# A state-space scan issued in rounds, with one bank pair for its decays and its gate units behind it

## The reference, cut to what matters

```python
def ssd_chunked(xs, dt, a, bm, cm):
    ...
    a_cs = jnp.cumsum(adt, axis=-1)
    seg = a_cs[..., :, None] - a_cs[..., None, :]
    decay_in = jnp.exp(jnp.where(tri, seg, -jnp.inf))
    cb = jnp.einsum("bclgn,bcsgn->bcgls", cc, bc)
    y_diag = jnp.einsum("bcgls,bcgrls,bcsgrp->bclgrp", cb, decay_in, xd)
    states = jnp.einsum("bclgn,bcgrl,bclgrp->bcgrpn", bc, decay_states, xd)
    def step(h, inp):
        st, dec = inp
        return h * dec[..., None, None] + st, h
    _, prev = lax.scan(step, h0, ...)
    y_off = jnp.einsum("bclgn,bcgrpn,bcgrl->bclgrp", cc, prev, jnp.exp(a_cs))
    return (y_diag + y_off).reshape(b, l, g, r, p)
...
y = y_fwd + y_bwd + d_skip * xs
return rms_norm(y * jax.nn.silu(z), ssd_norm)
```

## Time and profile before

| | us |
|---|---|
| median of 3 runs (lowest, highest) | 2350.87 (2345.1, 2355.63) |
| the profiled execution's own time | 2345.79 |
| its span, first to last instruction | 2344.0 |
| TensorE busy in the span | 2198.4 (94%) |
| ScalarE, VectorE, GpSimd busy | 1004.5, 1142.7, 962.0 |
| mean granted clock of TensorE, as a share of full speed | 0.961 |

### The profile page before, as it was taken

The page is one execution under the profiler, slowest core; times in us unless marked ns, Lnnn a source line. Parts: engine busy times, 40 slices in busy tenths (PEclk is TensorE's granted clock), DMA queues, the critical chain, the costliest instruction groups (busy, mean ns, idle before and its releaser), DMA issues.

```text
span 2344.0 us, 28202 instructions
## 1 busy us (share of the span) xinstructions
PE 2198.4 (94%) x10837; PEld 1826.0 (78%) x10848; DVE 1142.7 (49%) x1836; ACT 1004.5 (43%) x2027; POOL 962.0 (41%) x730
## 2 busy tenths in 40 slices
PE   7999899999988997899999998998899999999997
PEld 5788778888877776778888877785697887888886
DVE  3445565554344666465554363664445335544322
ACT  5666444443235555244443254655243234323222
POOL 3655553433457652444333442224323334322232
PEclk9999999999999999799999997998899999999998
DMA  4111122232213221122222221110012232222221
GB/s 157 55 55 60 49 99 99 90 108 99 94 60 102 82 68 39 62 82 90 98 100 97 88 88 36 37 36 19 19 46 101 88 108 72 92 106 90 101 99 52
DMA packets 29846, 183.08 MB, mean 78 GB/s; under 512 B 3984, under 2 KB 4112, under 8 KB 11920
## 3 DMA queue, kind: packets, MB, share of 16 engines
q1 hardware_dynamic: 29712, 181.27, 22.4%
HBM read 174.97 MB, written 2.10 MB: 76 GB/s over the span
## 4 chain that ended last, share of the span: by engine, by line
PE 82%; DVE 6%; ACT 5%; issue 3%; POOL 2%; DMA 1%; SPq 0%; POOLq 0%; ACTq 0%; DVEq 0%
PE PS L1452 81%; PE PS L1577 1%; POOL LO L2735 1%; DVE bQS L2191 1%; PE PS L1690 0%; ACT HI L1779 0%; DMA RAW<-wall 0%; DVE aQS L2191 0%; DVE T_f L2263 0%; DVE XL L2268 0%; DVE YH L2293 0%; PE PS L1625 0%; POOL cQ L2818 0%; ACT bP L1995 0%; POOL cROT L2810 0%
## 5 line engine op out<-in xcount | busy, mean ns | idle before, releaser
L2735 POOL TENSOR_TENSOR LO<-RAW,HI 128x512 fp32r<-128x512 f32 (+2 forms) x382 | 540.9, 1432 | 601.6 <-ACT HI L1779 601.3
L1452 PE MATMUL PS<-XH,HI 128*128 128x512 f32 (+1 forms) x1584 | 637.6, 403 | 24.5 <-DVE XL L2191 6.7
L1452 PE MATMUL PS<-XH,LO 128*128 128x512 f32 (+1 forms) x1584 | 624.4, 394 | 0.0
L1452 PE MATMUL PS<-XL,HI 128*128 128x512 f32 (+1 forms) x1584 | 618.1, 395 | 1.0 <-DVE XL L2268 1.0
L1779 ACT ACTIVATE HI<-RAW 128x512 fp32r<-128x512 f32 (+3 forms) x668 | 365.4, 608 | 171.3 <-PE PS L1452 168.0
L2191 DVE TENSOR_TENSOR LO<-RAW,HI 128x512 fp32r<-128x512 f32 (+2 forms) x286 | 305.0, 1071 | 246.2 <-ACT HI L1779 245.8
L1452 PEld LDWEIGHTS PS<-XH,HI 128*128 128x128 f32 (+1 forms) x1584 | 302.2, 191 | 87.7 <-issue 20.4
L1452 PEld LDWEIGHTS PS<-XH,LO 128*128 128x128 f32 (+1 forms) x1584 | 301.4, 190 | 65.7 <-issue 0.8
L1452 PEld LDWEIGHTS PS<-XL,HI 128*128 128x128 f32 (+1 forms) x1584 | 300.8, 190 | 62.7 <-DVE XL L2268 2.5
L1452 PE MATMUL PS<-HH,HI 128*128 128x512 f32 x528 | 205.4, 389 | 0.0
L1452 PE MATMUL PS<-HL,HI 128*128 128x512 f32 x528 | 205.4, 389 | 0.0
(11 more groups left out here) (395 smaller groups left out, 3358.3 us busy)
## 6 DMA issues: line engine op xcount, KB each, us to landing
RAW<-wall SPq DMA_DIRECT2D x138, 1024.0 KB, 4.8
RAW<-wall SPq DMA_DIRECT2D x24, 896.0 KB, 4.4
bROT<-bTQ SPq DMA_DIRECT2D x64, 64.0 KB, 2.0
RAW<-wall SPq DMA_DIRECT2D x5, 512.0 KB, 3.3
XF<-xT SPq DMA_DIRECT2D x4, 512.0 KB, 5.2
outT<-XR SPq DMA_DIRECT2D x8, 256.0 KB, 2.0
FP<-cfp SPq DMA_DIRECT2D x1, 1024.0 KB, 6.7
MKF<-cmask SPq DMA_DIRECT2D x1, 704.0 KB, 10.8
```

Source lines behind the costliest of these rows:

```text
L1452: return e.matmul(out, a, b, start=start, stop=stop)
L2735: return e.tensor_tensor(out, x, h.bitcast(F32), ALU.subtract)
```

## The change

The scan becomes one generator, `scan`, written in rounds. In round r the list has, in this order: `sw` and `sd` of state item r (on GpSimd), `sh` of head r, `sv` of item r - 2, `sq` of item r - 4, `sp` of item r - 1, `se` of head r, `so` of item r - 3, `em` of head r - 1, `sz` of head r - 3, `sy` of head r - 2, and up to four skip terms. So TensorE's order in a round is `sh`, `sp`, `so`, `sy`.

- The elementwise halves have become steps of their own: `se` is the exponentials of a head (was the second half of `sh`), `sz` the sum into `Y`, `sq` the scaling and sum of `so`, `sv` the copy or sum of a state, `sd` the decay of a state (was the second half of `sw`).
- The order of the 12 state items is a table, `STATES`, with two empty places.
- Banks: `sh` has 2 and 3 for every head, freed by `se` of the head before; `sp` has 4 or 5 by its direction, `so` has 6, `sy` stays in 7. Banks 0 and 1 are left to the dense units.
- The states of index 1 have a place of their own, `PR2`; the decay reads one place and writes the other, and no longer waits for `so` at that index. `so` waits for the state of its own group alone.
- `until` now advances the scan alone until the last `sq`, in round 17, by when all sixteen heads but the last sum are in the list. The z units come behind it. `opening`, `scans` and `PACE` are gone.

Instructions and their sizes are the same in number as before, and no DMA is added or taken away.

```diff
+STATES = ((0, 0, 0), (1, 0, 0), None, (0, 1, 0), (1, 1, 0), (0, 0, 1), (1, 0, 1), (0, 2, 0), (1, 2, 0), (0, 1, 1), (1, 1, 1), None,
+          (0, 2, 1), (1, 2, 1))
...
-    "sh": (("sm", 2), ("sem", 2)),
+    "sh": (("sm", 2),),
+    "se": (("sem", 2),),
     "em": (("smd", 1), ("smp", 1)),
-    "sy": (("sy", 1), ("syd", 1)),
-    "so": (("so", 1), ("sod", 1)),
+    "sy": (("sy", 1),),
+    "sz": (("syd", 1),),
+    "so": (("so", 1),),
+    "sq": (("sod", 1),),
     "sw": (("sxw", 1),),
+    "sd": (("sxw", 1),),
+    "sp": (("sst", 1),),
...
-        def head(h):
-            if h not in begun:
-                begun.add(h)
-                for dr in range(2):
-                    at_bank(("sh", h, dr), 2 + dr + 2 * (h % 2))
-                put("sh", h)
-                for dr in range(2):
-                    freed[2 + dr + 2 * (h % 2)] = ("sem", ("sh", h))
-                yield
-
-        def products(h):
-            if ("em", h) not in begun:
-                begun.add(("em", h))
-                put("em", h)
-            yield from ()
-
-        def sums(h):
-            if ("sy", h) not in begun:
-                begun.add(("sy", h))
-                s = ("sy", h)
-                at_bank(s, 7)
-                put(*s)
-                freed[7] = ("syd", s)
-                sdone[0] = h + 1
-                yield
-
...
-        def states(dr):
-            cs = (0, 1, 2, 3) if dr == 0 else (3, 2, 1, 0)
-            for idx, c in enumerate(cs):
-                if idx:
-                    for g in range(2):
-                        b, s = pick(), ("so", dr, idx, g)
-                        at_bank(s, b)
-                        put(*s)
-                        freed[b] = ("sod", s)
...
+        def scan():
+
...
+            def item(n):
+                return STATES[n] if 0 <= n < len(STATES) and STATES[n] else None
+
+            def skip_term(n):
+                for h in range(skipped[0], min(16, skipped[0] + n)):
+                    put("y0", h)
+                    skipped[0] = h + 1
+
+            r = 0
+            while sdone[0] < 16 or not finished[0]:
+                while item(r - 3) and ("cxt", CONV[-1]) not in steps:
                     yield
...
-                if idx < 3:
-                    for g in range(2):
-                        put("sw", dr, idx, g)
-                        yield
-                        b, s = pick(), ("sp", dr, idx, g)
-                        at_bank(s, b)
-                        put(*s)
-                        freed[b] = ("sprv" if idx else "sprv0", s)
-                        if idx == 0:
-                            yield
-            finished[dr] = True
...
-        def opening():
...
+                if item(r):
+                    put("sw", *item(r))
+                    if item(r)[1]:
+                        put("sd", *item(r))
+                if r < 16:
                     for dr in range(2):
-                        next(left[dr])
-                        yield
...
+                        at_bank(("sh", r, dr), 2 + dr)
+                    put("sh", r)
                     yield
-            for _ in range(2):
-                for dr in range(2):
-                    next(left[dr])
+                if item(r - 2):
+                    s = put("sv", *item(r - 2))
+                    freed[ag.bank_of[("sp",) + item(r - 2)]] = ("sprv" if s[2] else "sprv0", s)
+                if item(r - 4):
+                    dr, idx, g = item(r - 4)
+                    freed[6] = ("sod", put("sq", dr, idx + 1, g))
+                    finished[0] = r - 4 == len(STATES) - 1
+                if item(r - 1):
+                    s = ("sp",) + item(r - 1)
+                    at_bank(s, 4 + s[1])
+                    put(*s)
                     yield
-
...
-        def scans():
-            for n, _ in enumerate(staggered(list(range(16)), [head, products, sums], [0, 1, 2])):
-                yield
-                for i in range(PACE):
-                    next(left[(PACE * n + i) % 2], None)
...
+                if r < 16:
+                    s = put("se", r)
+                    for dr in range(2):
+                        freed[2 + dr] = ("sem", s)
+                if item(r - 3):
+                    dr, idx, g = item(r - 3)
+                    at_bank(put("so", dr, idx + 1, g), 6)
+                    yield
+                if 0 < r < 17:
+                    put("em", r - 1)
+                if 2 < r < 19:
+                    freed[7] = ("syd", put("sz", r - 3))
+                    sdone[0] = r - 2
+                if 1 < r < 18:
+                    at_bank(put("sy", r - 2), 7)
+                    yield
+                if ("cxt", 7) in steps:
+                    skip_term(4)
+                elif skipped[0] < 10:
+                    skip_term(2)
+                r += 1
...
-        first = opening()
-        while chores or together_chores:
-            chore()
-            next(first, None)
-        for _ in first:
-            pass
-        alongside(scans(), RATES[3])
-        until(lambda: sdone[0] >= 4 and all(finished))
+        alongside(scan(), RATES[3])
+        until(lambda: sdone[0] >= 4 and finished[0])
...
+    PR2 = [sb("cPR2a", 1024, F32, R0 + 113 * K), sb("cPR2b", 1024, F32, o2 + 28 * K)]
...
+    def state(dr, idx, g):
+        return blk(PR2[g], dr) if idx == 1 else blk(PRV, 2 * dr + g)
...
-                e.wait_ge(*when("sprv" if idx > 1 else "sprv0", "sp", dr, idx - 1, 1))
+                e.wait_ge(*when("sprv" if idx > 1 else "sprv0", "sv", dr, idx - 1, g))
                 s = 1024 + 512 * g + 128 * c
-                mm(PS[bank][:, :], BC[:, s:s + 128], blk(PRV, 2 * dr + g)).then_inc(SEM["so"], 1)
+                mm(PS[bank][:, :], BC[:, s:s + 128], state(dr, idx - 1, g)).then_inc(SEM["so"], 1)
...
-            elif kind == "sp" and a[1] == 0:
+            elif kind == "sv" and a[1] == 0:
                 dr, idx, g = a
-                e.wait_ge(*when("sst", *step))
-                act(blk(PRV, 2 * dr + g), PS[bank][:, :], ACT.Copy).then_inc(SEM["sprv0"], 1)
-            elif kind == "sh":
+                e.wait_ge(*when("sst", "sp", *a))
+                act(state(*a), PS[ag.bank_of[("sp",) + a]][:, :], ACT.Copy).then_inc(SEM["sprv0"], 1)
+            elif kind == "se":
                 h, = a
                 if h == 0:
                     e.wait_ge(*when("cdec", "cae"))
                 if h > 1:
                     e.wait_ge(*when("sy", "sy", h - 2))
                 for dr in range(2):
-                    e.wait_ge(SEM["sm"], when("sm", *step)[1] - 1 + dr)
+                    e.wait_ge(SEM["sm"], when("sm", "sh", h)[1] - 1 + dr)
...
-                e.wait_ge(SEM["sem"], when("sem", "sh", h)[1] - 1)
+                e.wait_ge(SEM["sem"], when("sem", "se", h)[1] - 1)
...
-            elif kind == "sy":
+            elif kind == "sz":
...
-            elif kind == "so":
+            elif kind == "sq":
...
-                e.wait_ge(*when("so", *step))
+                e.wait_ge(*when("so", "so", *a))
...
-            elif kind == "sp" and a[1]:
-                dr, idx, g = a
-                p = blk(PRV, 2 * dr + g)
-                e.wait_ge(*when("sst", *step))
-                e.wait_ge(*when("sxw", "sw", dr, idx, g))
-                e.tensor_tensor(p, p, PS[bank][:, :], ALU.add).then_inc(SEM["sprv"], 1)
+            elif kind == "sv" and a[1]:
+                p = state(*a)
+                e.wait_ge(*when("sst", "sp", *a))
+                e.wait_ge(*when("sxw", "sd", *a))
+                e.tensor_tensor(p, p, PS[ag.bank_of[("sp",) + a]][:, :], ALU.add).then_inc(SEM["sprv"], 1)
...
             elif kind == "sw":
...
-                if idx or g:
-                    e.wait_ge(*when("sst", "sp", dr, idx - (1 - g), 1 - g))
+                n = STATES.index(a)
+                before = [t for t in STATES[:n] if t and t[0] == dr]
+                if before:
+                    e.wait_ge(*when("sst", "sp", *before[-1]))
...
-                if idx:
-                    e.wait_ge(*when("so", "so", dr, idx, g))
-                    p = by8(blk(PRV, 2 * dr + g))
-                    m = e.tensor_tensor(p, p, CD[:, r:r + 8].unsqueeze(2).to_broadcast([128, 8, 64]), ALU.mult)
-                m.then_inc(SEM["sxw"], 1)
...
+            elif kind == "sd":
...
+                e.wait_ge(*when("sprv" if idx > 1 else "sprv0", "sv", dr, idx - 1, g))
+                if idx == 1:
+                    e.wait_ge(*when("cxm", "cxm", CONV[-1]))
+                    if g:
+                        e.wait_ge(*when("turn", "cxt", CONV[-1]))
+                else:
+                    e.wait_ge(*when("so", "so", dr, 1, g))
+                e.tensor_tensor(by8(state(*a)), by8(state(dr, idx - 1, g)), CD[:, r:r + 8].unsqueeze(2).to_broadcast([128, 8, 64]),
+                                ALU.mult).then_inc(SEM["sxw"], 1)
```

(61 more changed lines are left out.)

6 lines of the change are left out of this document (1 added, 5 removed).

## The result

The changed kernel takes 2404.44 us (median of 4 runs, 2399.83 to 2415.54) against 2349.38 for the kernel before (4 runs, 2345.10 to 2355.63). The ratio is 1.024, with a 95% interval of 1.020 to 1.028: 55 us slower. The prediction was 2398, range 2370 to 2422.

What follows compares the result with a forecast made beforehand. TensorE was taken to bound the kernel (82% of the span). Scan 150 + z 46.1 + 1 = 197 us in place of 147.2, +50 us, gave 2398 us, range 2370 to 2422.

Steps and rivals of the forecast that it cites:

- Where the time lies: Scan and z stages: 197 us in place of 147.2, +50 us.
- TensorE's work, 72.5 us at full clock: TensorE in the scan: sixteen heads and twelve of each state step take 72.5 us at full clock, 133.1 at half.
- The ring: TensorE and ScalarE in the scan: `sh` waits for `se`, which waits for `sy` last in TensorE's round; 36.8 us of gaps.
- The gap: TensorE between `sy` and the next `sh`: 2.18 + 0.17 + 0.16, together 2.5 us, paid in full by heads 3 to 15.
- The clock: TensorE in the scan: each gap costs 5.3 to 10 us of half clock; scan 150 us, mean clock about 0.65.
- The rule on bursts and waits: TensorE in the scan: bursts each followed by a long enough wait start at slow clock, tending to 171 us.
- z alone: z stage without heads: 46.1 us, plus about 1 us for first tiles at slow clock; late splits costed at nothing.
- Interleaving: Scan and z: mixing stages with different limits gains, and a repeating gap can mean too few buffers; both against the change.
- Elementwise steps and the second place, costed at nothing: VectorE 3.5 and GpSimd 3.6 us a round, hidden by the 7.5 us round; moved steps cost nothing.
- hidden exponentials: Rival for the scan: exponentials hide behind TensorE's work, rounds run back to back, 24 us gained, 2322 us; chance 0.04.
- Its decision point, a gap of 1.8 us at full clock: Gap before `sh`: below 1.8 us at full clock the change gains.
- All rounds at half clock: Rival for the scan: 171 us or a little more, +72 us and up, 2418 to 2425; chance 0.07 (or worse).

Runs made afterwards that it cites:

- the ring open: `sz` and `sy` moved to the front of each round, one bank pair kept, against the changed kernel: 2330.04 us, 0.9895 of the kernel before.
- the fill: Nine matmuls of 512 columns that nobody reads put behind the sum of rounds 2 to 14, against the changed kernel: 2363.4 us.
- z early: z let in from round 12, with its own gate buffer, against the kernel with the sum first in each round: 2341.21 us, 0.994 of before.

## Why the prediction was right, step by step

- **Where the time lies.** Right: the two stages, +55.0 us of the +55 between the medians. I had +50.
- **TensorE's work, 72.5 us at full clock.** Right: with the ring open the scan is 79.4 us, of which 3.0 are waits, at a clock of 0.95; a full round of 4.94 us against 3.13 + 1.87 = 5.0.
- **The ring.** Right, in its place, its two causes and its order: `sh` released by the exponentials, ScalarE by TensorE. Undoing either cause removes it.
- **The gap.** I had 2.5 us from start to start, of which 0.16 is `sy` running on and 2.18 + 0.17 = 2.35 is idle. The idle time was 2.27. I had thirteen full gaps; there were twelve, since head 3's is 1.82 us, and the waits for exponentials sum to 31.7 us. The last sums wait 0.55 and 0.57 us, for VectorE's addition that frees their bank and not, as I had it, for exponentials and product. In total I had 36.8 us of gaps; TensorE was idle for 154.83 - 119.55 = 35.3, all waits together, and the ring's price near full clock was 35.0.
- **The clock.** 0.62 against 0.65, and the scan 154.8 against 150, between the bounds of 145 and 171. All at full clock I had 110 us and a round of 7.5; the fill, with its clock at 0.94, showed 114.4 and 7.27. This was the step that I could least derive: "5.3 to 10 us of half clock for each wait" is a reading of two single waits, and 150 was picked between the ends, so that it came within 5 us is in part luck. In the full round shown above, 5.80 us and some 0.7 of `sy` ran at half clock, 6.5 us, nearer to the lower bound. The reading would have failed for a shorter wait: by the one of 1.81 us a wait of 1.2 should cost no clock, and in 4 of 11 rounds (1.28 us) and 10 of 12 (1.18 us) it did.
- **The rule on bursts and waits.** The Trainium skill, "TensorE: Matmul & The Clock Gate", section "HAM oscillation — how this bites in real kernels", was put as tending to the 171 us end. Here it agrees in kind: all twelve rounds behind 2.27 us had half clock in them, and eleven started with it. But the clock came back inside most rounds, so the stretch was at 0.62 and not at 0.50.
- **z alone.** 47.45 us against 46.1 + 1. No wait for a split: TensorE is busy for all of it.
- **Interleaving.** By the Trainium skill, "Perfetto Trace Analysis", section "Optimization Strategy", both the unmixed z and the single pair spoke against this change; of mixing the section says only that it may help. The runs part the two: too few buffers was true (65 us). Mixing was no gain where it was tried, with the ring open (z early is 8 us slower than z alone).
- **Elementwise steps and the second place, costed at nothing.** Right for this kernel (0.3 us), and for a reason that I hadn't given: the ring covers them. With the ring open the same step is 35 us. I should have named `em` as queued behind `sd` on GpSimd.
- **The rival "hidden exponentials", 24 us faster.** As a size it was right: the version in which they do hide is 147.3 - 125.5 = 21.8 us shorter in the stages. **Its decision point, a gap of 1.8 us at full clock, was wrong**: with a wait of 1.18 us the stages were 167.8 us, 20 above before. I had set it at full clock, which a recurring wait doesn't leave alone.
- **One slip in the sums.** All rounds at half clock make 171 + 46.1 + 1 - 147.2 = 70.9 us more, not 72. Nothing hangs on it.

## What to carry to other kernels

Walk each pair of waits between two engines through both in-order queues: if what frees the buffer stands last in the round of one and its successor first, the other engine's time is a gap in every round, and moving one step (here the sum, 77 us in the stages) or one more buffer opens it. Price such a gap twice, once as idle time and once as slow clock on the work around it; here the second part was the larger (40.4 against 35.0 us), and a run with useless matmuls in the gap parts the two. What an edit is worth in one order of the queue says nothing about another: the second state place was worth nothing that shows (0.3 us) with the sum last in the round and 35 us with it first.

## What the runs showed of the hardware that I had not expected

- A short wait that comes back costs clock in some rounds and not in others. Behind 2.27 us none of 12 rounds was wholly at full clock (0.62 over the scan), behind 1.18 us 2 of 12 (0.73), behind 1.28 us, in a longer round, 7 of 11 (0.81). One wait that costs nothing, like the one of 1.81 us before 5.02 us at 1.00, is no sign that the next one will cost nothing.
- Matmuls whose result nobody reads hold the clock about as well as real ones do: nine of 512 columns a round, 2.45 us, raised it from 0.62 to 0.94 (0.95 with the sum first and no filling) and made the round 3.0 us shorter.
- One exponential of 512 columns takes half the time of four of 128: 1.09 us for two against 2.18 for eight (the wide ones also leave out the bias tile).
